# Preparing the sample tile beside the last prompt tile, and two requests in flight in the sample phase

## The reference

```python
def _project(xn, shift_prev, w_in, mu_shift):
    p = jnp.einsum('bld,dc->blc', xn, w_in)
    pr, pm = p[..., :C_RWKV], p[..., C_RWKV:]
    prev = jnp.concatenate([shift_prev.astype(pr.dtype), pr[:, :-1]], axis=1)
    return pr + mu_shift * (prev - pr), pm, pr[:, -1:]
...
    w = jnp.exp(-DECAY_SCALE * jax.nn.sigmoid(decay_base + jnp.tanh(wd) @ w_decay_up))
    a = jax.nn.sigmoid(aaa_base + ad @ w_aaa_up)
    g = jax.nn.sigmoid(gd) @ w_gate_up
    kk = heads(k * k_k)
    kk = kk / jnp.maximum(jnp.sqrt(jnp.sum(kk * kk, -1, keepdims=True)), 1e-12)
    kt = k * (1.0 + (a - 1.0) * k_a)
...
    def step(S, inp):
        r_t, w_t, k_t, v_t, kk_t, a_t = inp
        sa = jnp.einsum('bhij,bhj->bhi', S, -kk_t)
        S = S * w_t[..., None, :] + sa[..., :, None] * (kk_t * a_t)[..., None, :] + v_t[..., :, None] * k_t[..., None, :]
        return S, jnp.einsum('bhij,bhj->bhi', S, r_t)
...
def _mla_attend(q_nope, q_rope, k_nope, k_rope, v, mask):
    s = jnp.einsum('bqhd,bkhd->bhqk', q_nope, k_nope) + jnp.einsum('bqhr,bkr->bhqk', q_rope, k_rope)
    p = jax.nn.softmax(s * ATTN_SCALE, axis=-1)
    return jnp.einsum('bhqk,bkhd->bqhd', p, v)
```

## Time and profile before

| | us |
|---|---|
| median of 3 runs | 2161.38 (2158.14 to 2174.07) |
| the profiled execution | 2160.93 |
| its span, first to last instruction | 2158.7 |
| mean granted TensorE clock | 0.938 |

### The profile page before, as it was taken

The page is one execution under the profiler, slowest core; times in us unless marked ns, Lnnn a source line. Parts: engine busy times, 40 slices in busy tenths (PEclk is TensorE's granted clock), DMA queues, the critical chain, the costliest instruction groups (busy, mean ns, idle before and its releaser), DMA issues. The chain is left out here.

```text
span 2158.7 us, 40158 instructions
## 1 busy us (share of the span) xinstructions
PE 1949.1 (90%) x16965; PEld 1667.8 (77%) x16965; DVE 950.1 (44%) x1852; ACT 666.6 (31%) x1300; POOL 357.6 (17%) x333
## 2 busy tenths in 40 slices
PE   6999977898889889897589799999999999999995
PEld 6999964676666666665377678999999999999994
DVE  7610114446575665553424255433354333543335
ACT  2221112234434444432201202333333333333331
POOL 0000014322332221210200032210102201022010
PEclk9999986688999999997779799999999999999998
DMA  6352111110211011000601632444444444444341
GB/s 216 134 196 87 43 42 46 43 43 4 73 56 55 2 56 55 2 14 11 176 2 21 235 108 60 125 128 125 127 122 140 143 119 133 121 140 143 119 134 39
DMA packets 168004, 196.38 MB, mean 91 GB/s; under 512 B 18770, under 2 KB 142570, under 8 KB 166692
## 3 DMA queue, kind: packets, MB, share of 16 engines
q1 hardware_dynamic: 165236, 184.84, 27.2%
q0 software_dynamic: 2624, 9.50, 1.1%
HBM read 165.88 MB, written 29.25 MB: 90 GB/s over the span
## 5 line engine op out<-in xcount | busy, mean ns | idle before, releaser
L664 DVE TENSOR_TENSOR c_wo_lo<-c_raw,c_wo_hi 128x1024 fp32r<-128x1024 f32 x96 | 117.6, 1225 | 465.8 <-ACT c_wo_hi L591 465.6
L803 PE MATMUL c_pY<-c_wo_hi,c_hl 128*128 128x512 f32 x576 | 226.0, 392 | 0.0
L803 PE MATMUL c_pY<-c_wo_lo,c_hh 128*128 128x512 f32 x576 | 225.8, 392 | 0.0
L803 PE MATMUL c_pY<-c_wo_hi,c_hh 128*128 128x512 f32 x576 | 225.2, 391 | 0.0
L591 ACT ACTIVATE c_wo_hi<-c_raw 128x1024 fp32r<-128x1024 f32 x96 | 101.8, 1061 | 332.1 <-PE c_pY L803 332.1
L547 POOL TENSOR_TENSOR c_hid<-c_relu 128x384 f32<-128x384 f32 x96 | 79.4, 828 | 677.2 <-ACT c_relu L606 677.2
L835 PE MATMUL c_pU<-c_zT_hi,c_wo_hi 128*128 128x384 f32 x768 | 151.2, 338 | 1.6 <-DVE c_zT_lo L659 1.6
L835 PE MATMUL c_pU<-c_zT_lo,c_wo_hi 128*128 128x384 f32 x768 | 148.6, 334 | 0.0
L835 PE MATMUL c_pU<-c_zT_hi,c_wo_lo 128*128 128x384 f32 x768 | 148.5, 334 | 0.0
L835 PEld LDWEIGHTS c_pU<-c_zT_hi,c_wo_hi 128*128 128x128 f32 x768 | 137.9, 188 | 9.7 <-DVE c_zT_lo L659 2.7
L835 PEld LDWEIGHTS c_pU<-c_zT_hi,c_wo_lo 128*128 128x128 f32 x768 | 134.5, 188 | 0.0
(11 more groups left out here) (471 smaller groups left out, 3481.4 us busy)
## 6 DMA issues: line engine op xcount, KB each, us to landing
c_raw<-w_down SPq DMA_DIRECT2D x96, 512.0 KB, 3.5
c_raw<-w_up SPq DMA_DIRECT2D x96, 512.0 KB, 4.7
scratch_p<-a_o SPq DMA_DIRECT2D x72, 154.0 KB, 1.8
a_w<-w_in SPq DMA_DIRECT2D x8, 1232.0 KB, 8.2
b_pr<-scratch_p SPq DMA_DIRECT2D x8, 1232.0 KB, 5.3
b_prev<-scratch_p SPq DMA_DIRECT2D x8, 896.0 KB, 4.6
scratch_h<-a_x POOLq DMA_DIRECT2D x9, 512.0 KB, 3.9
c_mix<-scratch_mix SPq DMA_DIRECT2D x9, 512.0 KB, 6.0
```

The lines of the kernel that those rows point to most:

```text
L664: dve.tensor_tensor(row_lo[U % 2], row_raw[U % 2][:, :], row_hi[U % 2].bitcast(F32), ALU.subtract).then_inc(S("row_lo"), 1)
L803: last = pe.matmul(pY[2 * t + half][:, :], x, w[:, 512 * half:512 * half + 512], start=first and a == 0, stop=final and a == 2, skip_group ...
```

## The change

1. Buffers that both the prompt phase (as the second of its two sets) and the sample phase use are allocated once for both: projections, shifted rows and decay factors, table, `a`, `kt`, `gate`, `bonus`, `wl`, latents, and a mask.
2. `schedule` prepares tile 9 beside tile 8 as far as `SAMPLE_AHEAD` goes: all but the latent's transposition, latent keys, values and queries. SP's `load(9)` reads the shifted rows from `prev` after the four shift copies; one mask is loaded in tile 3. `decay` uses the masks and exponents of the sample tile for tile 9.
3. The sample phase has no loads, shift, norm, LoRA, decay, keys or products any more. It starts with `turn_latent`.
4. Its list is new: the grams and the Newton steps come first, then scores 0 and 1, then per request `weights` v, `score` v+2, `context` v. `update` 0 and `mean` stand before request 4, `update` 1 and `variance` before request 5, `gate_out` before request 6.
5. All spins of the sample phase are gone.
6. ScalarE evicts the transposed weights instead of VectorE.
7. SP issues masks, weight, caches, state, new latents and then the other layout of the cache, with no wait on `c_ready`.

```diff
 def mix_weights_late(sb):
-    return {"q_norm_g": sb("m_q_norm_g", [P, Q_LORA])}
+    M = {n: sb(f"m_{n}", [P, W]) for n in ("a", "kt", "gate", "bonus")}
+    M.update({
+        "q_norm_g": sb("m_q_norm_g", [P, Q_LORA]), "pr": sb("m_pr", [P, C_IN]), "prev": sb("m_prev", [P, 4 * W]),
+        "table": sb("m_table", [P, 2 * ROPE]), "wl": sb("m_wl", [P, PAIRS, DEC_B]), "upper_eq_16": sb("m_upper_eq_16", [P, P]),
+        "c": sb("m_c", [P, KV_LORA]), "kr": sb("m_kr", [P, ROPE]), "qn": sb("m_qn", [P, Q_LORA]),
+    })
+    return M
...
+SAMPLE_AHEAD = ("shift", "norm", "lora", "turn_lora", "key_squares", "key_norm", "lora_up", "decay", "keys", "products")
...
+    ahead = lambda piece, i: [] if i > count else [(s, i, None) for s in piece if i < count or s in SAMPLE_AHEAD]
...
         beside = [[(s, i - 1, None) for s in (norm[m] if i > 1 else [])]
-                  + [(s, i + 1, None) for s in (prepare[m] if i + 1 < count else [])] for m in range(len(prepare))]
-        if vector and i + 1 < count:
+                  + ahead(prepare[m], i + 1) for m in range(len(prepare))]
+        if vector:
             beside[0] = [("shift_diff", i + 1, None)] + beside[0]
...
+                if i == NP:
+                    sp.wait_ge(S("shift_copied"), 16 * len(shifts))
+                sp.dma_start(prev[0:n, 0:C_RWKV], io["p"][t0:t0 + n, 0:C_RWKV] if i < NP else io["prev"])\
+                  .then_inc(S("prev_landed"), 16)
...
-                if i + 1 < NP:
-                    load(i + 1)
+                load(i + 1)
...
+    def attend(v):
+        return [("weights", v)] + [("score", v + 2)] * (v + 2 < DEC_B) + [("context", v)]
+
+    steps = plain("turn_latent", "queries", "turn", "gram") + [("newton_t", 0)] + plain("own") + [("newton_x", 0)]
+    steps += plain("turn_queries") + [("newton_t", 1)] + plain("absorb") + [("newton_x", 1)]
+    steps += [("score", 0), ("newton_t", 2), ("score", 1), ("newton_x", 2)] + plain("pick") + attend(0)
+    steps += plain("pick_turn") + attend(1) + plain("scan_sa") + attend(2) + plain("scan_y") + attend(3)
+    steps += [("update", 0)] + plain("mean") + attend(4) + [("update", 1)] + plain("variance") + attend(5)
+    return steps + plain("gate_out") + attend(6) + attend(7) + plain("values")
...
-            spins = {"turn_lora": 2, "lora_up": 2, "decay": 3, "absorb": 8, "turn": 6, "pick_turn": 2}
...
-                if step in spins:
-                    spin(pe, O[:, 0:P], ident, ident, spins[step])
-                if step in ("weights", "score"):
-                    spin(pe, O[:, 0:P], ident, ident, 5 if step == "weights" else 2)
-                if step == "context":
-                    spin(pe, O[:, 0:P], ident, ident, 3)
-                if step == "weights" and v >= 5:
-                    spin(pe, O[:, 0:P], ident, ident, 5 if v < 7 else 12)
...
-            sp.dma_start(pr[:, :], io["p"][1 + t0:1 + t0 + P, :]).then_inc(S("pr_landed"), 16)
-            sp.dma_start(prev[:, 0:C_RWKV], io["prev"]).then_inc(S("prev_landed"), 16)
-            sp.dma_start(table[:, :], io["table"][t0:t0 + P, :]).then_inc(S("table_landed"), 16)
...
+                if s == "weights":
+                    bank = J.take(act, ("PT", v))
+                    if v >= 2:
+                        act.wait_ge(S("s_filled"), J.number[("ctx", v - 2)] + 1)
+                    act.activation(PTb[v % 2][:, 0:2, :], bank[:, 0:2 * P].rearrange("p (k n) -> p k n", k=2), ACT.Copy)
+                    J.taken(act.activation(PTb[v % 2][0:T, 2, :], bank[0:T, 2 * P:3 * P], ACT.Copy), ("PT", v))
```

More of the change, by code:

```diff
@@ L1043, in schedule @@
         steps += attend("score", 0) + [("grams", i, None)]
-        steps += [("shift_diff", i + 1, None), ("squares", i + 1, None)] * (i + 1 < count and not vector)
+        steps += [("shift_diff", i + 1, None), ("squares", i + 1, None)] * (not vector)
         steps += attend("weights", 0) + attend("score", 1)
@@ L1092, in phase_mix_prompt @@
         la, lg = tmp[:, 0:LORA], tmp[:, LORA:LORA + P]
[L1093 removed]
+        a_, kt_, gate_, bonus_ = ([sb(f"b_{n}0", [P, W]), M[n]] for n in ("a", "kt", "gate", "bonus"))
         wl_ = [sb(f"b_wl{i}", [P, PAIRS, 2]) for i in range(2)]
@@ L1254, in _ @@
                     bank = J.fill(pe, (i, "total"))
+                    m0, m1 = (0, 2) if i < NP else (2, 2 + DEC_B)
                     for g in range(PAIRS):
-                        last = pe.matmul(bank[:, 2 * g:2 * g + 2], td[0:n, P * g:P * g + P], M["ind"][0:n, 0:2],
-                                         start=True, stop=True)
+                        last = pe.matmul(bank[:, (m1 - m0) * g:(m1 - m0) * (g + 1)], td[0:n, P * g:P * g + P],
+                                         M["ind"][0:n, m0:m1], start=True, stop=True)
                     J.filled(last)
@@ L2065, in _ @@
                         J.filled(last)
-                if step == "decay":
-                    pe.wait_ge(S("masks_landed"), 16)
-                    J.wait_taken(pe, "dec")
-                    for name, tri in (("inc", upper_eq), ("ex", upper)):
-                        bank = J.fill(pe, name)
-                        J.filled(pe.matmul(bank[:, :], tri, td[:, :], start=True, stop=True))
-                    bank = J.fill(pe, "total")
-                    for g in range(PAIRS):
-                        last = pe.matmul(bank[:, B * g:B * g + B], td[:, P * g:P * g + P], M["ind"][:, 2:10],
-                                         start=True, stop=True)
-                    J.filled(last)
                 if step == "turn":
                     for name, src in (("KT", w_ex), ("RT", w_inc), ("khT", kt), ("BT", a)):
-                        spin(pe, O[:, 0:P], ident, ident, 2)
-                        pe.wait_ge(S(f"{name}_src"), 1)
                         turns(name, lambda b: [(b[:, k * P:k * P + P], src[:, P * k:P * k + P]) for k in range(4)])
@@ L2254, in _ @@
             sp.dma_start(ropeT[:, :, 0:PAST], io["cache_ropeT"].rearrange("b r n -> r b n")).then_inc(S("ropeT_landed"), 16)
+            for g in range(PAIRS):
+                sp.dma_start(state[:, g, :, :], io["state"][:, P * g:P * g + P, :].rearrange("b p v -> p b v"))\
+                  .then_inc(S("state_landed"), 16)
+            for b in range(B):
+                sp.dma_start(lat_new[:, b, :], c[T * b:T * b + T, :]).then_inc(S("latnew_landed"), 16)
             sp.dma_start(lat[:, 0, :, :],
```

203 lines of the change are left out of this document (31 added, 172 removed).

## The result

| | before | after |
|---|---|---|
| median, us (8 runs each) | 2162.95 (2154.36 to 2174.07) | 2149.18 (2141.20 to 2150.73) |
| ratio | | 0.9933, interval 0.991 to 0.9956 |
| profiled execution | 2160.93 | 2147.14 |
| its span | 2158.7 | 2145.1 |
| mean granted TensorE clock | 0.938 | 0.925 |

The change saves 14 us, where 45 were forecast; 2149 lies above the forecast's range of 2095 to 2143. The three stretches of the profiled span add up to the difference of 13.6: up to the sample phase's first DMA +6.9 (1032.47 to 1039.36), the sample phase -21.6 (171.4 to 149.8 long), the MLP phase +1.1.

The account below looks back on a forecast made before the run. The prediction took TensorE's in-order queue, a third of it spins, to set the sample phase. From 2160.9 us, +1 for tile 8 and -46 for the sample phase gave 2116 us, range 2095 to 2143.

Parts of the forecast that it names:

- some 22 us of the 76 at half clock, + 17: Sample phase: granted clock about 0.7 to 0.75, so half-clock work adds 17 us, making 117 us.
- the 76 and the 1.75: Sample phase: TensorE's remaining work is 76 us at full clock; at half clock it takes 1.75 times as long.
- A third of the queue is padding: Sample phase: 50.2 of TensorE's 137.0 busy us are spins, matmuls whose result nobody reads.
- 4.3 stay: Sample phase: TensorE's issue gaps among the tiny matmuls, three of 1.3 to 1.6 us, remain at 4.3 us.
- rival C: Sample phase: TensorE waits for caches and state at first score and state products; kernel 2136 us, chance 0.06.
- The waits of 5 and 7: Sample phase: TensorE waits 5 and 7 us because VectorE's updates, mean and variance precede normalisation of requests 4 and 5.
- the four items: Sample phase: waits at the start, issue gaps, VectorE's order, and last evictions with gating; together 23 to 24 us.
- Evictions at no cost: Sample phase: the two evictions moved to ScalarE, 0.7 us a request, fit under the 1.7 us score, cost 0.
- +1, bounds -3 and +8: Prompt tile 8: net change +1 us, between ending 6 us earlier and 4 to 8 us later.
- some 6: Prompt tile 8: added LoRA turns, three up-projections and two decay sums take TensorE some 6 us at full clock.
- the side engines cost nothing: Prompt tile 8: added preparation on VectorE (18 us), ScalarE (10) and POOL (17) costs nothing, hidden behind the heads.
- A: Sample phase: half clock nearly throughout, phase 149 us, prompt +5, kernel 2152 us; chance 0.10.

Follow-up runs that it names:

- experiment 3: Changed kernel, with SP loading state and latents only once TensorE has filled the second transposed Newton product: 2130.79 us, ratio 0.9853, phase 137.5 us.
- experiment 4: Changed kernel, with VectorE normalising requests 4, 5 and 6 ahead of updates, mean, variance and gating: 2137.19 us, ratio 0.9877, phase 139.3 us.
- 6: Changed kernel, but with the old order of the sample steps, still without spins: 2137.40 us, ratio 0.9895.
- the first kernel of 7: Changed kernel with both the late loads of state and latents and VectorE's earlier normalisations: 2124.62 us, ratio 0.9835, phase 125.7 us.
- Experiment 1: Two kernels: kernel before with only the preparation moved beside tile 8, 2139.32 us (0.9888); kernel before with only its sample spins removed, 2175.77 us (1.006).
- experiment 5: Changed kernel with VectorE evictions, 2149.07 us; old order with preparation moved and spins, plus ScalarE evictions, 2138.04 us; that plus two requests in flight, 2130.18 us.
- experiment 2: Changed kernel with 128 of the old sample-phase spins put back at the same steps: 2152.71 us, ratio 0.9942, phase 155.7 us.

## Why the prediction was wrong

The profiled execution came out at 2147.1 against 2116. By its own terms, the miss of 31 is 24.7 in the sample phase (141.7 against 117), 6.1 in tile 8 and 1.1 in the MLP phase, less 0.8 in the stretches between these and by rounding.

**The step that failed: "some 22 us of the 76 at half clock, + 17".** It was 49 us of the 76, and + 37. The changed kernel's phase has six stretches at a granted clock of 0.50. Windows over them give, for the last one up to the end of TensorE's work and for all together:

```profile
1131.82:1181.13 49.31, 35.36 (x168) 26.72 (x168) 14.65 (x38) 5.45 (x17) 1.26 (x1) 0.50 0.09 22
...
sum 112.28, PE 85.75 PEld 66.63 DVE 21.66 ACT 15.20 POOL 1.26; mean PE 12.25 PEld 9.52 DVE 3.09 ACT 2.17 POOL 0.18
```

By the prediction's own factor of 1.75 the 85.7 us busy are 49.0 of work, and with the 27.6 us busy at full clock they make 76.6. So the 76 and the 1.75 were right; worked out in the same way, the four experiments without spins on this work (3, 4, 6 and the first kernel of 7) and the one with VectorE evictions give 76.0 to 77.2. Only the part of the work that falls to the lower level was mis-sized. 113.3 less 76 is 37, and 37 less 17 is 20 of the 24.7; idle time is the other 4.4. The term fitted its own clock: 22 us of work stretch to 39, and with all 24 of waits the lower level holds 63 of 117 us, a mean clock of 0.73. It was that clock, 0.70 to 0.75, which had no row behind it: tile 8 at 0.82, or the sample phase at 0.86, had spins or denser work in their gaps. Experiment 1 gives the row that was missing, a sample phase without spins at 0.58; the measured 0.63 is near it. "A third of the queue is padding" was read as time to be saved, and spins that hold the clock are not that.

**The issue gaps: "4.3 stay".** There were 10.2. With the loads moved 4.9 remain, so the term was nearly right for the instructions and wrong for what ran beside them: each gap is a wait for a block of code, and the loads made one block late (experiment 3). The prediction kept the loads as hidden because no step waits for their data, and its rival C looked for a wait on data. No such wait came: the loads cost 12.3 us of the phase (experiment 3) without releasing one instruction, 5.3 in gaps and 7.3 in busy time. This belongs partly to the first step: the idle gap stands right before a fall of the clock.

**The waits of 5 and 7** were right in place and cause, 4.8 and 8.1; the kind of removal that the mechanism asks for (experiment 4) takes them away. All idle time between start and end was 28.4, against the 22.8 that the four items add up to ("23 to 24"): 5.9 more in issue gaps, 0.9 in these two waits and 1.4 ahead of another request, less 1.3 at the start and 1.4 at the end.

**Evictions at no cost**: right as far as the intervals can tell, on both orders (experiment 5). A reading that changes nothing: "VectorE is never more than half busy" is slightly off, 19.99 of 37.75 us in its densest window.

**Tile 8: +1, bounds -3 and +8.** It took 84.6 us instead of 77.5: +7.1, at the upper bound. ScalarE's timeline after has the seventh head's exponential 60.5 us into the tile; it was 53.2 before, so +7.3 where 4 was read:

```profile
994.43 1.11 ACT L1706 ACTIVATE b_P<-b_SC,b_nb 128x1024 f32<-128x1024 f32 x1 [4.71 <-DVE b_nb L1896]
```

TensorE's groups in the tile show why: the up-projections, decay sums and turns ("some 6") come to 7.0 us by the sum of their rows, and two waits are new, 1.8 and 1.6 us:

```profile
L1209 PE MATMUL b_R<-b_XA,b_F 64*64 64x64 f32 x128 | 4.6, 221 | 1.6 <-DVE b_F L1847 1.6
L1209 PE MATMUL b_R<-b_IA,b_XA 64*64 64x64 f32 x128 | 4.5, 219 | 1.8 <-ACT m_prev L1645 1.8
```

The prediction then took +1 as a value between an end 6 us earlier, with the slow stretch gone, and one up to 8 later; the stretch stayed. That the side engines cost nothing is nearly right: 1.8 us for ScalarE's decay exponentials in front of a Newton product. This was read from the trace; no experiment tested it alone.

**Of the rivals**, A (half clock nearly throughout, 2152) came nearest, with a clock of 0.63, a kernel at 2149 and a phase of 141.7 against its 149. It had a chance of 0.10 and deserved the larger part.

What stays open: why the clock falls during the state products, although TensorE is not idle there; why the late block of code was late; and how the 7 us of tile 8 split between its waits and its work.

## What to carry to other kernels

Price spins by a run or a stretch without them, never by their busy time: here 50 us of them hid 24 of waits and saved 41 by the clock. A forecast clock wants a row of the same kind of work without its spins; turned into time at the lower level, (1 - c) / 0.5 of the stretch, it can be held against a trace (0.63 of 149.8 us is 111, and 112.3 were found). After a reordering, look at each engine's own queue behind the long step (a normalisation behind an update). Count the instructions of small products, since every 128 matmul records with their weight loads use up a block of code, and keep large transfers away from them. The repairs of experiments 3 and 4 took 24 us out of the phase, the whole change 22.

## What was unexpected of the hardware

- Loads that nobody waits for stopped TensorE for 5.2 us and cost the phase 12.3. A block of code came 8.1 us after the one before, instead of 4.2 (experiment 3).
- The clock fell to 0.50 inside the 256 records of state products of 64x16, without idle time before. In the kernel of experiment 2 TensorE was busy without a break from 1072.9 us on, at 1.00; the products began at 1085.6, and the clock fell at 1089.9:

```profile
1072.88:1085.62 12.74, 12.74 (x317) 10.72 (x309) 3.74 (x10) 3.35 (x7) 0.00 (x0) 1.00 0.01 3
1085.62:1089.93 4.31, 4.31 (x150) 4.31 (x149) 0.43 (x2) 1.21 (x4) 0.00 (x0) 1.00 0.01 4
1089.93:1096.00 6.07, 6.07 (x116) 6.03 (x112) 0.00 (x0) 0.28 (x2) 0.00 (x0) 0.50 0.01 3
```

It fell 2 to 6 us into these products in 12 of the 14 kernels; in the other two it was at 0.50 already. The first 128 records took 3.9 us where the clock was 1.00 throughout, the same number 7.0 at 0.50. The rule that the prediction cited, from "TensorE: Matmul & The Clock Gate" of the Trainium skill, Part 1 ("The HAM clock gate"), speaks of an idle array; here the array was not idle when the clock fell.

- 25 spins of 128 columns, put where waits had stood, raised the phase's clock from 0.70 to 0.80 and shortened it by 7.8 us.
